# A two-block transformer forward pass on one core: the norm ahead of layer a made one, norm sums and spreads set apart, a new order of the begin, and the gate columns as weights

## What is computed

```python
n = rms_norm(h, attn_norm_w); proj = n @ w_in        # first block
a, b = gate columns of proj (8 columns)              # g and beta of the delta net
h = h + mix @ w_out
h = h + conv_glu_mlp(rms_norm(h, mlp_norm_w))
x = rms_norm(h, final_norm_w)                        # norm 2
x = x + attention_a(rms_norm(x, norm_mix_g[0]))      # norm 3, second block
x = x + mlp(rms_norm(x, norm_mlp_g[0]))
...
y = rms_norm(x, norm_final_g)
```

## Time and profile before

| | us |
|---|---|
| three runs, median | 2168.53 |
| lowest and highest | 2165.61, 2170.63 |
| profiled execution, its own time | 2170.82 |
| its span in the profile | 2168.9 |
| mean granted clock, share of 2.4 GHz | 0.965 |

### The profile page before, as it was taken

One profiled execution on the slowest core, in us unless ns is written; L12 is line 12 of the kernel. 1 busy time (PEld: TensorE's weight loads), 2 busy tenths in 40 slices (PEclk: granted clock), 3 DMA queues, 4 the chain that ended last, 5 costly groups with the idle time before them and its releaser, 6 DMA issues.

```text
span 2168.9 us, 25396 instructions
## 1 busy us (share of the span) xinstructions
PE 2085.1 (96%) x9454; PEld 1659.4 (77%) x9454; DVE 1031.0 (48%) x1400; ACT 768.4 (35%) x953; POOL 165.8 (8%) x146
## 2 busy tenths in 40 slices
PE   6999899899999999899899999999999989999998
PEld 5878788778888877687778888888666568888887
DVE  5743632346754765434554323424665644423433
ACT  3352132244532434215643312313454543312322
POOL 2010141010000002700010000002000010000001
PEclk9989987799999999999999999999999999999999
DMA  8635201023223223622013233224222113322221
GB/s 197 87 54 78 78 1 39 1 78 97 87 87 115 80 72 102 134 96 60 1 59 97 97 97 97 87 88 133 93 92 76 56 41 96 97 97 89 87 95 58
DMA packets 161477, 177.72 MB, mean 82 GB/s; under 512 B 3998, under 2 KB 156820, under 8 KB 161268
## 3 DMA queue, kind: packets, MB, share of 16 engines
q1 hardware_dynamic: 157392, 160.64, 25.9%
q0 software_dynamic: 3808, 15.94, 2.7%
q10 hardware_dynamic: 196, 0.06, 0.0%
HBM read 174.43 MB, written 2.20 MB: 81 GB/s over the span
## 4 chain that ended last, share of the span: by engine, by line
PE 76%; DVE 3%; ACT 2%; issue 1%; POOL 0%; DVEq 0%; ACTq 0%
PE bank L704 23%; PE bank L705 22%; PE bank L706 22%; PE bank L793 2%; PE bank L989 1%; PE bank L1108 1%; PE bank L1121 1%; PE bank L1011 1%; PE bank L786 1%; PE bank L768 1%; DVE w_lo L1199 1%; ACT w_hi L1194 0%; PE bank L981 0%; DVE a_q L2007 0%; DVE ff_lo L1907 0%
## 5 line engine op out<-in xcount | busy, mean ns | idle before, releaser
L704 PE MATMUL bank<-n_hi,w_hi 128*128 128x512 f32 x1504 | 614.7, 409 | 10.7 <-DVE w_lo L1199 5.3
L1194 ACT ACTIVATE w_hi<-raw 128x2048 fp32r<-128x2048 f32 x154 | 295.1, 1917 | 915.6 <-PE bank L706 913.1
L705 PE MATMUL bank<-n_lo,w_hi 128*128 128x512 f32 x1504 | 599.8, 399 | 0.0
L706 PE MATMUL bank<-n_hi,w_lo 128*128 128x512 f32 x1504 | 599.1, 398 | 0.0
L1199 DVE TENSOR_TENSOR w_lo<-raw,w_hi 128x2048 fp32r<-128x2048 f32 x154 | 358.7, 2329 | 314.1 <-ACT w_hi L1194 312.6
L704 PEld LDWEIGHTS bank<-n_hi,w_hi 128*128 128x128 f32 x1504 | 286.0, 190 | 103.3 <-issue 37.5
L704 PE MATMUL bank<-ff_hi,w_hi 128*128 128x512 f32 x848 | 338.7, 399 | 7.3 <-DVE ff_lo L1907 2.5
L705 PEld LDWEIGHTS bank<-n_lo,w_hi 128*128 128x128 f32 x1504 | 286.0, 190 | 70.1 <-issue 4.6
L706 PEld LDWEIGHTS bank<-n_hi,w_lo 128*128 128x128 f32 x1504 | 285.6, 190 | 70.2
L705 PE MATMUL bank<-ff_lo,w_hi 128*128 128x512 f32 x848 | 335.9, 396 | 0.0
L706 PE MATMUL bank<-ff_hi,w_lo 128*128 128x512 f32 x848 | 335.8, 396 | 0.0
(11 more groups left out here) (294 smaller groups left out, 1836.7 us busy)
## 6 DMA issues: line engine op xcount, KB each, us to landing
raw<-in_mlp_w_in SPq DMA_DIRECT2D x32, 1024.0 KB, 5.5
raw<-in_mlp_w_out SPq DMA_DIRECT2D x32, 1024.0 KB, 5.1
raw<-in_w_up SPq DMA_DIRECT2D x22, 1024.0 KB, 5.1
raw<-in_w_in SPq DMA_DIRECT2D x16, 1024.0 KB, 9.8
raw<-in_a_w_qkv SPq DMA_DIRECT2D x12, 1024.0 KB, 5.2
raw<-in_b_w_qkv SPq DMA_DIRECT2D x12, 1024.0 KB, 5.2
b_bias<-bias_table POOLq DMA_DIRECT2D x16, 448.0 KB, 5.4
raw<-in_w_down SPq DMA_DIRECT2D x8, 768.0 KB, 4.5
```

What stands on the lines that cost most here:

```text
L704: nc.tensor.matmul(b[:, :], w_hi[:, j % 2, cols], hi, start=start, stop=False)
L705: nc.tensor.matmul(b[:, :], w_hi[:, j % 2, cols], lo, start=False, stop=False)
L706: return nc.tensor.matmul(b[:, :], w_lo[:, j % 2, cols], hi, start=False, stop=final)
L1194: act.activation(w_hi[:, s, :], raw[:, s, :], ACT.Copy).then_inc(hi_ready, 1)
```

## The change

- The begin. TensorE transposes the parameter rows first, then x (now in a place of its own, x_first). ScalarE loads its table ahead, makes n_hi tile by tile as x comes, and splits unit 0 in two halves ahead of n_hi of tile 3. VectorE makes n_lo between its copies and its w_lo in two halves. TensorE starts on the first half. POOL's loads wait until unit 0 has landed.
- Sums and spread of the norms 0, 1, 4, 5, 6 are apart: the sums stay behind the first unit, the spread comes six products into the second.
- Norms 2 and 3 are one: TensorE makes sum(h^2) and sum(w^2 h^2) from one set of squares, with a right side of two columns (two_sums), eight matmuls behind every second k of tile 0 of the second unit. From both VectorE and ScalarE make both roots; they are spread nine products into tile 1. POOL has no part in it. hT is scaled in place behind the phases q and k.
- The gate columns are the weights: 16 matmuls with 512 tokens moving, giving rows; VectorE copies them (ab_rows), and behind the first unit of p_gate four small transposes turn them. The third bias product, the sums of the gates and ScalarE's gate functions move there too.

```diff
         ring = []
-        ring += [("x", f) for f in range(4)] + [("par",)] + [("x", f) for f in range(4, KD)]
-        ring += norm_ring(0) + [("ffn0",), ("ab",)] + [("bias", n) for n in range(RB_COLS // SEQ)] + [("gc",)]
+        ring += [("par",)] + [("x", f) for f in range(KD)]
+        ring += norm_ring(0) + [("ffn0",), ("ab",), ("bias", 0), ("bias", 1), ("ab_turned",), ("bias", 2), ("gc",)]
...
         ring += [("rms", 0)] + [("rms_b", n) for n in range(4)] + [("x_again", f) for f in range(4, KD)]
         ring += norm_ring(1)
...
         def _(pool):
+            pool.wait_ge(w_loaded[0], 16)
             pool.dma_start(ab_raw[:, :, :], t["w_in"][0].rearrange("(k p) n -> p k n", p=P)[:, :, 2048:2056])\
...
             pool.dma_start(rel_bias[:, :], t["rel_bias_2"]).then_inc(at("bias_in"), 16)
-            pool.wait_ge(x_loaded[1], 16)
             pool.dma_start(consts[:, FIRST_CONSTS:CONST_COLS], t["consts"][:, FIRST_CONSTS:CONST_COLS]).then_inc(rest_loaded, 16)
...
             pool.wait_ge(at("bias_stored"), 16)
-            norm_pool(pool, 2)
-            norm_pool(pool, 3)
             attention_a_pool(pool)
...
+                        first = by_tile and ph.u0 + j == 0
+                        if first:
+                            pe.wait_ge(at("first_lo"), 1)
+                        else:
+                            pe.wait_ge(lo_ready, it * ph.per + ph.u0 + j + 1)
                         at_last = ph.upg * ph.kt - 1
                         if by_tile and j == 0:
                             for i, k in enumerate(order):
+                                if first and k == KD // 2:
+                                    pe.wait_ge(lo_ready, 1)
...
                                     ins = three(j, g, tile, k, src, src == 0, src == at_last)
-                                if tile == 0 and q == ph.upg - 1:
-                                    ins.then_inc(tile0_ready, 1)
+                                    if tile == 0 and src == at_last:
+                                        ins.then_inc(tile0_ready, 1)
+                                    if by_tile and norm is not None:
+                                        norm_between(pe, norm, tile, k)
                         ins.then_inc(w_used, 1)
-                        if by_tile and j < len(norms):
-                            norm_tensor(pe, norms[j])
+                        if by_tile and j == 0 and norm not in (None, 2):
+                            norm_sums(pe, norm)
...
+        def norm_spread(pe, n):
+
+            pe.wait_ge(norm_r, NORM[n] + 1)
             spread(pe, ("norm_b", n), r_model, 0)
+            if n == 2:
+                spread(pe, ("norm_b", 3), r_head, 0)
+
+        def two_sums_of(pe, c):
+
+            b = ring_slot(("norm", 2))[0]
+            if c == 0:
+                ring_group(pe, ("norm", 2))
+                pe.wait_ge(norm_sq, 3 * NORM[2] + 3)
+            for f in range(KD):
+                ins = nc.tensor.matmul(b[:, 2 * c:2 * c + 2], scratch[:, f, c * P:(c + 1) * P], two_sums[:, f, :],
+                                       start=f == 0, stop=f == KD - 1)
+            if c == TOK - 1:
+                ring_filled(ins)
+
+
+        def norm_between(pe, n, tile, k):
+
+            if n == 2 and tile == 0 and k % 2 == 1:
+                two_sums_of(pe, k // 2)
+            if (tile, k) == ((1, 2) if n == 2 else (0, 1)):
+                norm_spread(pe, n)
...
                 if step == 2 * KD - 1:
-                    norm_tensor(pe, 5)
+                    norm_sums(pe, 5)
+                elif step == 2 * KD + 1:
+                    norm_spread(pe, 5)
...
+            pe.wait_ge(rows_loaded, 16 * len(PAR_ROWS))
+            b = ring_group(pe, ("par",))
+            ring_filled(nc.tensor.transpose(b[:, 0:PAR_N], par_rows[0:PAR_N, :], ident[0:PAR_N, 0:PAR_N]))
             for f in range(KD):
                 pe.wait_ge(x_loaded[f // 4], 16)
-                if f == 4:
-                    pe.wait_ge(rows_loaded, 16 * len(PAR_ROWS))
-                    b = ring_group(pe, ("par",))
-                    ring_filled(nc.tensor.transpose(b[:, 0:PAR_N], par_rows[0:PAR_N, :], ident[0:PAR_N, 0:PAR_N]))
-                four_transposes(pe, ("x", f), lambda c: x_rows[:, c, f * P:(f + 1) * P])
-            project(pe, p_conv, N_HI, N_LO, (norm_lo, 0), (0,))
+                four_transposes(pe, ("x", f), lambda c: x_first[:, c, f * P:(f + 1) * P])
+            project(pe, p_conv, N_HI, N_LO, (norm_lo, 0), 0)
...
             b = ring_group(pe, ("ab",))
-            for c in range(TOK):
-                for k in range(KD):
-                    n = slice(c * P, (c + 1) * P)
-                    o = b[:, 16 * c:16 * c + 16]
-                    nc.tensor.matmul(o, n_hi[:, k, n], ab_both[:, k, :], start=k == 0, stop=False)
-                    ins = nc.tensor.matmul(o[:, 0:8], n_lo[:, k, n], ab_hi[:, k, :], start=False, stop=k == KD - 1)
+            for k in range(KD):
+                nc.tensor.matmul(b[0:16, :], ab_both[:, k, :], n_hi[:, k, :], start=k == 0, stop=False)
+                ins = nc.tensor.matmul(b[0:8, :], ab_hi[:, k, :], n_lo[:, k, :], start=False, stop=k == KD - 1)
...
+            def bias_products(n):
                 b = ring_group(pe, ("bias", n))
                 ring_filled(nc.tensor.matmul(b[0:HEADS, :], rel_bias[:, :], one_hot[:, n * SEQ:(n + 1) * SEQ], start=True, stop=True))
-            project(pe, p_gate, N_HI, N_LO)
-
+
+            def gates_turned():
+                b = ring_group(pe, ("ab_turned",))
+                ring_taken(pe, ("ab",))
+                for c in range(TOK):
+                    ins = nc.tensor.transpose(b[:, 16 * c:16 * c + 16], ab_rows[:, c * P:(c + 1) * P], ident[0:16, 0:16])
+                ring_filled(ins)
+                bias_products(2)
+
+            bias_products(0)
+            bias_products(1)
+            project(pe, p_gate, N_HI, N_LO, between=gates_turned)
...
+        def first_split_hi(act):
+            act.wait_ge(w_loaded[0], 16)
+            done(act, act.activation(w_hi[:, 0, FIRST[0]], raw[:, 0, FIRST[0]], ACT.Copy), at("first_hi"), 1)
+            done(act, act.activation(w_hi[:, 0, FIRST[1]], raw[:, 0, FIRST[1]], ACT.Copy), hi_ready, 1)
+
+        def first_split_lo(dve, half):
+            ready, left = ((at("first_hi"), at("first_lo")), (hi_ready, lo_ready))[half]
+            dve.wait_ge(ready, 1)
+            done(dve, dve.tensor_tensor(w_lo[:, 0, FIRST[half]], raw[:, 0, FIRST[half]], w_hi[:, 0, FIRST[half]].bitcast(F32),
+                                        ALU.subtract), left, 1)
...
-                residual_part(act, n, part)
+                if n:
+                    residual_part(act, n, part)
                 if n in SPLIT:
                     for f in range(a, b):
+                        if n == 0:
+                            ring_taken(act, ("x", f))
+                        if n == 0 and f == 3:
+                            first_split_hi(act)
                         done(act, act.activation(n_hi[:, f, :], hT[:, f, :], ACT.Copy, scale=input_weight(n, f)),
                              norm_hi, KD * SPLIT[n] + f + 1)
...
             own_act(act, act.activation(act_mark[:, :], eps, ACT.Sqrt))
             next_split(act, n, split_hi, 1)
+            if n == 2:
+                ring_taken(act, ("norm", 2))
+                done(act, act.activation(r_cols[:, 0:2 * TOK], r_cols[:, 0:2 * TOK], ACT.Sqrt), at("two_roots"), 1)
+                return
...
+            if n == 2:
+                next_split(dve, n, split_lo, 1)
+                two_norms_vector(dve)
+                return
...
+        def two_norms_vector(dve):
+            b = ring_read(dve, ("norm", 2))
+            mean = b[:, 0:2 * TOK].rearrange("p (c n) -> p n c", n=2)
+            own_dve(dve, dve.tensor_scalar(r_model, mean[:, 0, :], EPS, None, ALU.add))
+            ring_done(dve, dve.scalar_tensor_tensor(r_head[:, 0:TOK], r_model, EPS, mean[:, 1, :], ALU.mult, ALU.add), ("norm", 2))
+            dve.wait_ge(at("two_roots"), 1)
+            r = r_cols[:, 0:2 * TOK]
+            done(dve, dve.reciprocal(r, r), norm_r, NORM[2] + 1)
+            b = ring_read(dve, ("norm_b", 3))
+            ring_done(dve, dve.tensor_copy(rstd[:, :], b[:, :]), ("norm_b", 3))
+
+        def in_place(dve, tiles):
+            b = ring_read(dve, ("norm_b", 2))
+            for f in tiles:
+                ins = dve.scalar_tensor_tensor(hT[:, f, :], hT[:, f, :], par_col("final_norm", f), b[:, :], ALU.mult, ALU.mult)
+                if f < KD - 1:
+                    done(dve, ins, h_ready, f + 1)
+                else:
+                    ring_done(dve, ins, ("norm_b", 2))
+                    done(dve, dve.tensor_copy(b_mark[:, 0:1], b_mark[:, 1:2]), h_ready, KD)
...
+        def gates_scalar(act):
...
-            next_split(act, 0, split_hi, 0)
+            own_act(act, act.activation(act_mark[:, :], eps, ACT.Copy))
             ring_taken(act, ("par",))
```

(50 more changed lines are left out.)

88 lines of the change are left out of this document (40 added, 48 removed).

## The result

The changed kernel takes 2136.78 us (median of 4 runs, 2135.41 to 2140.68); the kernel before took 2169.58 in the same rounds. The ratio is 0.985, with a 95% interval of 0.9825 to 0.9876: faster by 32.8 us. The forecast was 2140, with a range of 2129 to 2156. The profiled execution took 2135.73 us, 35.1 less than the profiled one of before.

What follows compares the result with a forecast made beforehand. The prediction took the order of work on TensorE as the bound. Begin 5.0, gates 9.3, norms 5.4 and joint norm 9.0 sum to 28.7 us, giving 2140 for a median run; range 2129 to 2156.

Steps and rivals of the forecast that it cites:

- The bound, and the places: Whole kernel: bound by the order of work on TensorE, with gains at begin, gates, norms between stages and joint norm.
- The begin: Start of the kernel: first product at 17.5, unit 1 near 36; 5.0 us won, from 0.5 to 9.
- Rival (c): Begin: transposes running into the products bring the clock up, 2.5 us of half clock go; 2137.5, chance 0.08.
- The gates: Gate products: 16 wide matmuls replace 64 narrow ones; 9.3 us won, from 6.5 to 11.3.
- rival (d): Gates: g is late, ScalarE's three table loads end after TensorE's 2 us margin; up to 4 us, 2144, chance 0.08.
- Norms 1, 4, 5 and 6: Norms between stages: wait of 0.70 hidden at two, 2.2 and 2.3 saved at the others; 5.4 us taken.
- The joint norm: Norms 2 and 3 made one: TensorE then waits 2.0 for w_lo; 9.0 us won, from 7.0 to 9.8.
- 32 sums (twice 1.84): Joint norm: its 32 sums on TensorE costed at twice 1.84, 3.7 us.
- (a): Begin: the loads don't come sooner, something else held them; begin gives 1, time 2144, chance 0.13.
- (b): Norm sums and gates: narrow groups keep pulling the clock down; 21 us won, time 2147.5, chance 0.16.
- (e): Six norm places: each loses the clock for its whole next unit; slower, 27 above, 2196, chance 0.03.
- (f): New places: n_lo or bank order makes TensorE wait as at the old ones; within 4 us of before, chance 0.02.

Runs made afterwards that it cites:

- narrow-product run: Changed kernel with the 64 narrow gate products again instead of the 16 wide ones, and no turning: 2146.76 us.
- spread run: Changed kernel with the spread of norms 0, 1, 4, 5 and 6 right behind their sums again: 2146.4 us.
- The rounded squares: Changed kernel with the joint norm's squares and two columns of weights written as fp32r, making its 32 sums fp32r matmuls: 2134.84 us.
- the two other executions: The changed kernel itself, nothing altered, profiled twice more as the mark for other runs: 2138.07 and 2138.38 us.

## Why the prediction was right, and where it was not

**The bound, and the places.** Right. The chain is TensorE's, and all gains lie at the places named.

**The begin** (5.0 forecast, 7.75 measured). The landings held: parameter rows 8.97 for 9.5, and unit 0 there by 13.68, when ScalarE splits it, for 13.5. Three terms failed. The transposes: I took 0.9 a group, from 16 in 3.62 us. Those 16 stood 0.213 us apart, the pace of half clock, which I did not see. In the changed kernel the clock rose among them, the later ones stood 0.109 apart, and all 32 took 5.36 us; so the first product came at 16.17, not 17.5. The clock: I left 2.5 us of half clock behind the transposes, and there was none. Rival (c) held, to which I had given 0.08: the transposes do bring the clock up. The fall in the kernel before was the work of the 5.3 us of pause ahead of its first product; I read the 0.77 of that product and not the stretch ahead of it. The Trainium skill (TensorE: Matmul & The Clock Gate, Part 4: PE-mode transpose) says that full clock doesn't engage for them. The traces decide otherwise: the clock rose at 12.66 with nothing but transposes on TensorE since 8.97, and in all thirteen traces of the changed kernel and its variants their distance falls from 0.213 to 0.109 where the record of 1.00 begins (12.32 to 18.98). GpSimd: I had its adds at 9.1 us and TensorE waiting 2.7 for them. They took 6.9, because VectorE waited instead, and TensorE waited 3.4 for n_lo. I saw the contention and put its price on the wrong engine. No clock was lost behind the sums (1.1 had been taken).

**The gates** (9.3, 10.84). The working gave 11.3 and I took 2.0 off for a clock that might not hold, by the bias products' row. That row was misread: those products ran at 0.50 because the narrow ones had brought the clock down; the narrow-product run shows it. The margin for g was 0.9 instead of 2.0, so rival (d) was near.

**Norms 1, 4, 5 and 6** (5.4, 6.16). Right in mechanism and size; 0.8 at the two that I had at 0.70, and 2.2 and 2.3 as worked out. But "the clock fell at 5 and 6 and not at 1 and 4" is not a property of these norms, as the spread run shows.

**The joint norm** (9.0, 5.66). The mechanism was right, down to the wait for w_lo (1.82 for 2.0) and what stands in it. The term mis-sized is "32 sums (twice 1.84)": the third unit of q starts 4.67 earlier where I had 8.2. The row of before has x16 for the eight matmuls of a norm: an fp32 matmul stands as two records. Thirty-two are 64 records, 7.4 us and not 3.7. The rounded squares show the other size, 3.8. Behind that product the clock gave 1.66, where I had 1.1. The last 0.68 went at 887, where a split meets GpSimd's 8.3 us add; the two other executions don't lose it. The scaling in place stands behind that split (from 887.36) and costs TensorE nothing that these traces show, as forecast.

**The sum.** Begin, gates and norms were 5.0 under, the joint norm 3.3 over; 4.6 more came from stretches that the change does not touch. That the forecast is only 3 above the median is in part luck: the errors cancel. Of the rivals (c) held; (a), (b), (d), (e) and (f) are out; no unit behind a norm ran at half clock as a whole.

## What to carry to other kernels

Before a row is multiplied, its count is divided by the instructions in the code: here one fp32 matmul is two records (a transpose and an fp32r matmul are one), and a term was half of what it cost. Before a pace is carried over, it is asked at which clock it was measured; the distance of the starts says it where the record of the clock has not begun. Narrow matmuls cost least in short groups between products (1.84 us here), or turned so that the wide operand moves. And an add on GpSimd is charged to VectorE's two-input work beside it: each waits for the other's whole instruction.
